# The up-projections of four squared-ReLU MLPs as seven block products in place of eight

## What is computed

```
D_MODEL = 1024; SEQ = 512; DEPTH = 4; D_FF = 4 * D_MODEL
def _squared_relu_mlp(h, w1, w2):
    return jnp.square(jax.nn.relu(h @ w1)) @ w2
for i in range(DEPTH):
    ...                                   # x = x + mixer(rmsnorm(x))
    x = x + _squared_relu_mlp(_rmsnorm(x, norm_mlp[i]), mlp_w1[i], mlp_w2[i])
```

## Time and profile before

| | us |
|---|---|
| median of the timed runs (3) | 2053.24 |
| lowest, highest | 2053.15, 2054.11 |
| profiled execution: its span, first to last instruction | 2050.5 |
| TensorE busy | 2041.0 |
| VectorE busy | 1175.2 |
| ScalarE busy | 839.1 |

### The profile page before, as it was taken

One profiled execution on the slowest core, in us unless ns is written; L12 is line 12 of the kernel. 1 busy time (PEld: TensorE's weight loads), 2 busy tenths in 40 slices (PEclk: granted clock), 3 DMA queues, 4 the chain that ended last, 5 costly groups with the idle time before them and its releaser, 6 DMA issues.

```text
span 2050.5 us, 25188 instructions
## 1 busy us (share of the span) xinstructions
PE 2041.0 (100%) x9744; PEld 1688.5 (82%) x9744; DVE 1175.2 (57%) x1426; ACT 839.1 (41%) x1208; POOL 232.8 (11%) x323
## 2 busy tenths in 40 slices
PE   9999999999999999999999999999999999999998
PEld 7888888888878888888888888888888888888887
DVE  7865544443897735344598754434477756435344
ACT  7654322323466523132356532222347644132233
POOL 7002000000200200004431200000721011000000
PEclk9999999999999999999999999999999999999999
DMA  6122232323323232322332333232332122232331
GB/s 196 55 67 93 94 101 92 102 92 98 105 75 103 93 103 92 102 92 95 100 87 69 95 101 102 92 102 94 105 93 71 62 93 93 94 100 92 102 103 52
DMA packets 123875, 192.47 MB, mean 94 GB/s; under 512 B 17713, under 2 KB 37745, under 8 KB 123793
## 3 DMA queue, kind: packets, MB, share of 16 engines
q1 hardware_dynamic: 116848, 186.04, 28.3%
q0 software_dynamic: 4544, 3.94, 0.7%
q10 hardware_dynamic: 2400, 1.38, 0.2%
HBM read 185.30 MB, written 2.10 MB: 91 GB/s over the span
## 4 chain that ended last, share of the span: by engine, by line
PE 98%; DVE 1%; ACT 0%; DMA 0%; SPq 0%; issue 0%
PE psum L584 30%; PE psum L585 30%; PE psum L586 30%; PE psum L984 2%; PE psum L957 1%; PE psum L1092 1%; PE psum L933 1%; PE psum L929 0%; PE psum L928 0%; PE psum L934 0%; PE psum L927 0%; PE psum L1194 0%; PE psum L1224 0%; PE psum L1210 0%; DMA x<-in_x 0%; ACT arena L2677 0%
## 5 line engine op out<-in xcount | busy, mean ns | idle before, releaser
L1348 DVE TENSOR_TENSOR w_lo<-w_raw,w_hi 128x1024 fp32r<-128x1024 f32 x339 | 417.9, 1236 | 742.5 <-ACT w_hi L2171 741.9
L2171 ACT ACTIVATE w_hi<-w_raw 128x1024 fp32r<-128x1024 f32 x343 | 362.9, 1061 | 933.5 <-PE psum L586 933.4
L584 PE MATMUL psum<-h_hi,w_hi 128*128 128x512 f32 x1368 | 535.6, 392 | 1.1 <-DVE w_lo L1348 1.1
L585 PE MATMUL psum<-h_lo,w_hi 128*128 128x512 f32 x1368 | 532.4, 389 | 0.0
L586 PE MATMUL psum<-h_hi,w_lo 128*128 128x512 f32 x1368 | 532.4, 389 | 0.0
L584 PE MATMUL psum<-u_hi,w_hi 128*128 128x512 f32 x1256 | 492.0, 392 | 0.1
L586 PE MATMUL psum<-u_hi,w_lo 128*128 128x512 f32 x1256 | 489.1, 389 | 0.0
L585 PE MATMUL psum<-u_lo,w_hi 128*128 128x512 f32 x1256 | 488.9, 389 | 0.0
L584 PEld LDWEIGHTS psum<-h_hi,w_hi 128*128 128x128 f32 x1368 | 256.8, 188 | 55.9 <-DVE w_lo L1348 1.5
L586 PEld LDWEIGHTS psum<-h_hi,w_lo 128*128 128x128 f32 x1368 | 256.8, 188 | 53.6
L585 PEld LDWEIGHTS psum<-h_lo,w_hi 128*128 128x128 f32 x1368 | 256.9, 188 | 53.5 <-issue 1.2
(11 more groups left out here) (291 smaller groups left out, 1627.4 us busy)
## 6 DMA issues: line engine op xcount, KB each, us to landing
w_raw<-in_mlp_w SPq DMA_DIRECT2D x256, 512.0 KB, 3.7
w_raw<-in_mla_w_o SPq DMA_DIRECT2D x16, 512.0 KB, 3.5
w_raw<-in_lru_w_in SPq DMA_DIRECT2D x16, 512.0 KB, 3.9
w_raw<-in_swa_w_in SPq DMA_DIRECT2D x12, 512.0 KB, 3.9
w_raw<-in_mla_w_ukv SPq DMA_DIRECT2D x8, 512.0 KB, 4.9
w_raw<-in_lru_w_out SPq DMA_DIRECT2D x8, 512.0 KB, 3.4
w_raw<-in_swa_w_o SPq DMA_DIRECT2D x8, 512.0 KB, 3.8
w_raw<-in_mla_w_in SPq DMA_DIRECT2D x7, 512.0 KB, 3.7
```

What stands on the lines that cost most here:

```text
L584: nc.tensor.matmul(out, stat[0], mov[0], start=start, stop=False, skip_group_check=skip)
L585: nc.tensor.matmul(out, stat[0], mov[1], start=False, stop=False, skip_group_check=skip)
L1348: ins = nc.vector.tensor_tensor(w_lo[:, to], w_raw[:, to], exact(w_hi[:, to]), ALU.subtract)
L2171: nc.scalar.activation(w_hi[:, to], w_raw[:, to], ACT.Copy).then_inc(w_hi_done, 1)
```

## The change

The eight up groups of an MLP are one as before (the first, `up(0)` of slice 0) and seven in the new form, 28 in the kernel. A new group splits the weights (as W transposed: output features by inputs) in 2x2 blocks A of 256 output features by 512 inputs, and h in 2x2 blocks H of 512 inputs by 256 tokens. Seven products of a sum of A blocks with a sum of H blocks are made (`seven_products`), each 24 matmuls of 256 columns:

| product | weights | tokens | into |
|---|---|---|---|
| 1 | A11 | H11 | xy, bank 0 |
| 2 | A11+A21 | T3 | own, bank 0 |
| 3 | A11+A21+A22 | T2 | xy, bank 0, added |
| 4 | A12 | H21 | xy, bank 1 |
| 5 | A21+A22 | T1 | xy, bank 0, added |
| 6 | A22 | T4 | own, bank 0, added |
| 7 | all four | H22 | xy, bank 0, added |

xy and own are areas 0 and 1 for g = 0, 2 and 3 for g = 1. Between products ScalarE copies a bank to the arena (c11 after product 1, c22 after 2, c21 after 3; the four chunks lie where `relu` and `scaled` lie) and VectorE adds or subtracts there. The four sums of weights are made in place in the raw tiles by VectorE, right behind the low part of the block that was there before. T1 to T4 are made once per layer from a scaled copy of x in the upper halves of u_hi and u_lo, and split in high and low parts. The squares of the new groups are made on ScalarE. w1 is loaded as blocks of 512 rows by 256 columns; two slots in the arena (4 and 5) are added to the four, for MLP units only, and their loads wait for the layer's last h. The hardware loops are written out. h lies in memory by blocks in the MLPs.

The core of the diff:

```diff
+    def seven(i, at):
+        nonlocal sums
+        a, q, e, b = (Raw(("w1_block", i, half, at + n, BLOCK), phase, True)
+                      for half, n in ((0, 0), (0, HALF), (1, HALF), (1, 0)))
+        raws.extend((a, q, e, b))
+        ops.append(Operand("A11", a, (q,)))
+        ops.append(Operand("A11+A21", a, (e, q), made=sums + 1))
+        ops.append(Operand("A11+A21+A22", a, made=sums + 2))
+        ops.append(Operand("A12", b, (a,)))
+        ops.append(Operand("A21+A22", q, made=sums + 3))
+        q.freed = len(ops)
+        ops.append(Operand("A22", e))
+        e.freed = len(ops)
+        ops.append(Operand("A11+A12+A21+A22", b, made=sums + 4))
+        a.freed = b.freed = len(ops)
+        sums += 4
...
-                need(sp, w_ready, c.at("unit", 1 - SLOTS))
-                to = w_raw[:, slot * UNIT:slot * UNIT + u[-1]]
+            def load():
+                raw = raws[c.now("raw")]
+                u, landed = raw.unit, w_loaded[raw.slot]
+                need(sp, w_ready, raw.after)
+                if raw.slot >= SLOTS:
+                    sp.wait_ge(h_ready, KC * (raw.phase + 1))
+                to = raw_tile(raw)
...
+            def units_of_u(kp):
+                pe.wait_ge(u_ready, c.now("u_ready") + (2 if kp < 2 else 4))
             def down(g):
-                def ready(kp):
-                    pe.wait_ge(u_ready, c.at("u_ready", kp + 1))
-                square_group((0, 1) if g == 0 else (2, 3), UHI, ULO, ready if g == 0 else anything)
+                square_group((0, 1) if g == 0 else (2, 3), UHI, ULO, units_of_u if g == 0 else anything)
                 if g == 1:
                     c.add("u_ready", 4)
-            def mlp(last):
-                up(0, {3: norm_sums(2)}, h_chunks)
+            def seven_products(g, layer):
+                xy, own = (0, 1) if g == 0 else (2, 3)
+                r = c.now("rounds")
+                c.add("rounds")
+                def group(to, tokens, begun):
+                    next_unit_ready()
+                    wh, wl = unit()
+                    for m in range(2):
+                        for k in range(4):
+                            at = slice(k * HALF + m * P, k * HALF + (m + 1) * P)
+                            kt = slice(k * HALF, (k + 1) * HALF)
+                            mm = product(to[:, m * HALF:(m + 1) * HALF], (wh[:, at], wl[:, at]),
+                                         (tokens[0][:, kt], tokens[1][:, kt]), not begun and m == k == 0,
+                                         m == 1 and k == 3, skip=True)
+                    mm.then_inc(unit_done, 1)
+                    c.add("tensor_unit")
+                claim(xy)
+                group(bank(xy, 0), H11, False)
+                claim(own)
+                jobs["round", r] = c.now(f"area{xy}"), c.now(f"area{own}")
+                pe.wait_ge(turned_ready, 4 * layer + 2)
+                group(bank(own, 0), T3, False)
+                pe.wait_ge(c_copied, 3 * r + 1)
+                pe.wait_ge(turned_ready, 4 * layer + 3)
+                group(bank(xy, 0), T2, True)
+                group(bank(xy, 1), H21, False)
+                pe.wait_ge(c_copied, 3 * r + 3)
+                group(bank(xy, 0), T1, True)
+                pe.wait_ge(turned_ready, 4 * layer + 4)
+                group(bank(own, 0), T4, True)
+                pe.wait_ge(c_added, 2 * r + 2)
+                group(bank(xy, 0), H22, True)
+            def mlp(layer, last):
+                square_group((0, 1), BLOCK_HI, BLOCK_LO, h_chunks, {3: norm_sums(2)}, blocks=True)
                 c.add("h", 8)
-                with pe.Fori(0, TURNS) as turn:
-                    c.begin(turn)
-                    up(1)
-                    down(0)
-                    down(1)
-                    up(0)
-                    c.end(TURNS)
-                up(1)
-                if last:
-                    down_by_rows()
-                else:
-                    down(0)
-                    down(1)
+                for s in range(SLICES):
+                    if s:
+                        seven_products(0, layer)
+                    seven_products(1, layer)
+                    if last and s + 1 == SLICES:
+                        down_by_rows()
+                    else:
+                        down(0)
+                        down(1)
...
+                    if op.role == "A11":
+                        a21, = op.others
+                        dve.wait_ge(w_loaded[a21.slot], a21.landed)
+                        nc.vector.tensor_tensor(tile, tile, raw_tile(a21), ALU.add).then_inc(sums_made, 1)
+                    elif op.role == "A11+A21":
+                        a22, a21 = op.others
+                        dve.wait_ge(w_loaded[a22.slot], a22.landed)
+                        nc.vector.tensor_tensor(tile, tile, raw_tile(a22), ALU.add).then_inc(sums_made, 1)
+                        nc.vector.tensor_tensor(raw_tile(a21), raw_tile(a21), raw_tile(a22), ALU.add
+                                                ).then_inc(sums_made, 1)
+                    elif op.role == "A12":
+                        others, = op.others
+                        nc.vector.tensor_tensor(tile, tile, raw_tile(others), ALU.add).then_inc(sums_made, 1)
...
+            def u_lo_of(g, j):
+                c.add("u_hi")
+                dve.wait_ge(u_hi_done, c.now("u_hi"))
+                block = (first_tokens, other_tokens)[j]
+                nc.vector.tensor_tensor(tokens_of(u_lo, g, j), by_chunk(block), exact(tokens_of(u_hi, g, j)),
+                                        ALU.subtract).then_inc(u_ready, 1)
+            def seven_products(g):
+                xy, own = (0, 1) if g == 0 else (2, 3)
+                r = c.now("rounds")
+                c.add("rounds")
+                c.add("tensor_unit", 3)
+                split(1)
+                if g == 1 and r % 7:
+                    u_lo_of(0, 1)
+                split(2)
+                product_passed()
+                dve.wait_ge(c_copied, 3 * r + 1)
+                nc.vector.tensor_tensor(c11, bank(xy, 1), c11, ALU.add).then_inc(c_added, 1)
+                split(1)
+                product_passed()
+                dve.wait_ge(c_copied, 3 * r + 2)
+                nc.vector.tensor_tensor(c22, c22, bank(xy, 0), ALU.subtract).then_inc(c_added, 1)
+                split(1)
+                product_passed()
+                dve.wait_ge(c_copied, 3 * r + 3)
+                free(nc.vector.tensor_tensor(c21, bank(own, 0), c21, ALU.subtract), own)
+                split(1)
+                u_lo_of(g, 0)
+                c.add("tensor_unit")
+                split(1)
+                c.add(f"area{xy}")
...
             def mlp(gain):
+                c.add("gained", 4)
+                dve.wait_ge(gained_done, c.now("gained"))
+                nc.vector.tensor_tensor(b11, b11, b12, ALU.subtract).then_inc(turned_made, 1)
+                c.add("gained", 4)
+                dve.wait_ge(gained_done, c.now("gained"))
+                nc.vector.tensor_tensor(b12, b12, b22, ALU.subtract).then_inc(turned_made, 1)
                 sums_lo()
-                split(3)
+                split(1)
+                turned_lo(T1, b11)
+                turned_lo(T3, b12)
+                nc.vector.scalar_tensor_tensor(out=b11, in0=b11, scalar=-1.0, in1=b22, op0=ALU.mult,
+                                               op1=ALU.subtract).then_inc(turned_made, 1)
+                split(1)
+                turned_lo(T2, b11)
+                nc.vector.tensor_tensor(b21, b21, b11, ALU.add).then_inc(turned_made, 1)
+                split(1)
                 norm_rows()
                 link(nc.vector.tensor_tensor(rstd2[:, :], rstd[:, :], rstd[:, :], ALU.mult))
                 split(1)
-                with dve.Fori(0, TURNS) as turn:
-                    c.begin(turn)
-                    squared_relu(0)
-                    split(4)
-                    squared_relu(1)
+                squared_relu(0)
+                turned_lo(T4, b21)
+                for s in range(SLICES):
+                    if s:
+                        seven_products(0)
+                    seven_products(1)
+                    u_lo_of(1, 1)
+                    if s + 1 == SLICES:
+                        break
...
+            def u_hi_of(g, j):
+                block = (first_tokens, other_tokens)[j]
+                link(nc.scalar.activation(block, block, ACT.Square))
+                nc.scalar.activation(tokens_of(u_hi, g, j), by_chunk(block), ACT.Copy).then_inc(u_hi_done, 1)
+            def seven_products(g):
+                xy, own = (0, 1) if g == 0 else (2, 3)
+                r = c.now("rounds")
+                c.add("rounds")
+                product_passed()
+                act.wait_ge(u_ready, c.now("u_ready") - 1)
+                need(act, x_ready, c.now("x_ready") - 1)
+                nc.scalar.activation(c11, bank(xy, 0), ACT.Copy).then_inc(c_copied, 1)
+                split(1)
```

(69 more changed lines are left out.)

293 lines of the change are left out of this document (174 added, 119 removed).

## The result

The changed kernel takes 2117.85 us (median of 4 runs, 2115.34 to 2120.06), the kernel before 2053.19 beside it: **3.15% slower**, ratio 1.0315 with the interval [1.03, 1.0329]. The prediction, 2101 us in the range 2060 to 2140, holds in sign and range and is 17 us short.

The account below looks back on a forecast made before the run. TensorE, busy 2041.0 of 2050.5 us, was taken as the bound. Per layer -11.2 + 12.3 + 9.0 + 1.8 = +11.9, four layers +47.6; 2050.5 + 47.6 + 2.7 = 2100.8, so 2101 us, range 2060 to 2140.

Parts of the forecast that it names:

- Matmuls, -11.2 per layer: Seven up groups per layer: 168 matmuls spaced 0.120 us replace 96 at 0.2267, gaining 1.60 us a group, 11.2 per layer.
- Rival (c): 256-column matmuls in the new stream are spaced wider, 0.19 us, for the weight load: 2380 us; chance 3%.
- Start of a layer, 12.3 us of waiting: At each layer's first MLP slice TensorE waits 12.3 us in two pieces, ahead of the first and third products.
- The wait for area 2: At a layer's start, ahead of the first product, TensorE waits about 4.2 us until norm_rows frees area 2.
- the one ahead of the third product: At a layer's start TensorE waits 8.1 us for ScalarE's copy of the first product's bank.
- Later slices, 9.0 per layer: Third products in later slices wait 1.1 us in first groups and 1.9 in second, three each per layer: 9.0 us.
- The two chains named: Later slices: VectorE's scaled sum, x and copy (1.1 us late); ScalarE's relu, square, u_hi row before the copy (1.9).
- The clock, 1.8 per layer: TensorE restarts slowly behind the 8 us pause at a layer's start: 1.8 us per layer, bounds 0 and 3.6.
- Costed at nothing: Weight loads, loop branches and strided writes of h and u add nothing; unhidden loads at a layer's start up to 2 us.
- its upper end, 2135: Full instruction durations, hand-overs of 0.1 us and 1.9 us for loads give 20.5 us per layer, 2135 us.
- Rival (a): Everything beside TensorE is hidden, so only the 11.2 us gained per layer show: 2008 us, faster; chance 4%.

Follow-up runs that it names:

- sq_only: Changed kernel with c11 and c21 in sq, c11's copy ahead of u's high parts, one VectorE low part of u earlier; 2053.07 us, 1.0001 of the kernel before.
- both2: Changed kernel with c11's copy early, the norm's reciprocal and Newton step late, c22 and c21 copied earlier in each layer's first round; 2011.41 us, 0.9797 of the kernel before.

## Right and wrong, step by step

- **Matmuls, -11.2 per layer: right.** Spacing 0.120; with the waits at 4.4 us, 2053.1 - 44.8 + 4.4 = 2012.7 against 2011.4 measured. Rival (c), wider spacing, is out. The Trainium skill (TensorE: Matmul & The Clock Gate, Back-to-back issue gap) has prices from which the prediction estimated 98 ns at 256 columns and a longer group; the measured 0.120 us at 256 and 0.2267 at 512 don't agree with them.
- **Start of a layer, 12.3 us of waiting: 10.7 measured.** The times of the results are right to 0.1 us (the spacing of 1.15 us is 1.14 by its own two rows, too little to show in eleven of them). The wait for area 2 was 3.9 to 5.3 us (4.2 expected), the one ahead of the third product 5.9 to 6.4 (8.1): TensorE came to that one at 227.11 - 6.39 - 0.65 = 220.1, not at 226.6 - 8.1 = 218.5, since its first two products ran partly at half clock (0.79 in 212 to 220). That loss hid in the wait.
- **Later slices, 9.0 per layer: 8.4 measured** (33.4 in all; 1.01 and 1.76 to 1.95 for 1.1 and 1.9). The two chains named, add_scaled and the copy in shared memory for g = 0, ScalarE's row of relu, square, u_hi for g = 1, are the ones that sq_only broke.
- **The clock, 1.8 per layer: mis-sized, about 8.4 (33.5 / 4).** This is the failed step: four times 6.6 is 26 us too few, of which the two terms above take 9 back, and 17 are left. It lies outside the bounds set for it too (0 and 3.6). It was put down once per layer, "behind a pause of 8 us", and taken from the 4.80 us of the first 24 matmuls, not from a wait in the midst of work, of which the trace of before has none to show. The waits of 1.9 us, three per layer, were given none, and the eleven low stretches behind them make 19 of the 33.5 us. The prediction cited the Trainium skill (TensorE: Matmul & The Clock Gate, HAM oscillation) for idle gaps that restart the engine at half clock and set it aside because the page of before reads nine tenths everywhere. But before there are no pauses of that kind, so that row couldn't speak against it; the trace of the changed kernel agrees with it at the layers' starts, where waits of 3.9 to 6.4 us go with 10 to 14 us at half clock. It shows half clock behind waits of 1.8 us too, which are shorter than the 3 to 5 us of the Trainium skill's example there, and none behind those of 1.0 us.
- **Costed at nothing: right.** Blocks of weights land in 3.9 and 4.7 us, and the table of waits has none of TensorE for a block (ScalarE waited for one three times, 3.8 us in all):

```profile
w_raw<-in_mlp_w SPq DMA_DIRECT2D x176, 512.0 KB, 3.9
arena<-in_mlp_w SPq DMA_DIRECT2D x80, 512.0 KB, 4.7
```

- **The sum.** Predicted for four layers: -44.8 + 49.2 + 36.0 + 7.2 = +47.6. Measured: -44.8 + 42.6 + 33.4 + 33.5 = +64.7. Two terms were 9 us too high together, one 26 too low. That 2118 still lies in the range is luck in part: its upper end, 2135, was made of longer chains and late loads, and the waits came out shorter than forecast. Rival (a), all hidden, 2008, is what both2 comes to by another order: the point named as decisive, c11's copy there within two products, is the one that had to be mended.

## What to carry to other kernels

A change that shortens TensorE's stream and lengthens the chains beside it is worth its columns only if every result is there in time: here 45 us of columns drew 76 us of waits and 33 of clock, and three moves in the order of ScalarE and VectorE gave back 106.5 of these 109 us. Follow each buffer of such a chain to the last user of its memory; c11 was late for what else lay there and stood ahead of it in the queue, not for its own work. And price a wait of TensorE of nearly 2 us or more at up to twice its length (here 1.76 us and 1.7 behind it), one of up to 1.4 us at little more than its length (twelve of 0.76 us left 0.3 us each beside it).

## What the chip did that I had not expected

- Waits of 1.76 to 1.95 us were followed by 3.4 us at 0.50 granted clock in 11 of 12 cases of the changed kernel; 36 pauses and 12 waits of 0.8 to 1.4 us by none. In the changed kernel the stretch begins 0.2 to 1.5 us after TensorE's restart, so it costs 1.7 us of work that runs, not of the wait.
- Whether a pause of 1.8 to 2.4 us brings one is not fixed by the program: one and the same kernel, with pauses of 2.43 us, spread over 11 us for it (2092.07 to 2103.20), where the kernel before, run beside it, spreads over 1.4.
- 64.7 us of loss are all but invisible in the page's clock row (one 8 among nines). The mean clock of the core, 0.980 against 0.999, and windows of a few us behind each wait show it.
